# Loading most expert weight chunks as two transfers of 64 partitions in place of one of 128

## The reference

```
def expert_choice_ffn(x, router_w, wg, wu, wd):
    cap = CAPACITY_FACTOR * n // N_EXPERTS            # 32 tokens for each of 16 experts
    aff = softmax(x @ router_w); gate, idx = top_k(aff.T, cap)
    xg = x[idx]
    hid = silu(xg @ wg[e]) * (xg @ wu[e])             # 32 x 1024, for every expert e
    o = (hid @ wd[e]) * gate
    return zeros_like(x).at[idx].add(o)
```

## Time and profile before

| what | value |
|---|---|
| median of three runs | 2420.06 us |
| the profiled execution's own time | 2413.2 us |
| its span, first to last instruction | 2411.4 us |
| TensorE busy | 2212.5 us, 92% of the span |
| mean rate of all transfers over the span | 274 GB/s |
| TensorE's mean granted clock | 0.992 of full speed |
| moved | 660.65 MB |

### The profile page before, as it was taken

One profiled execution on the slowest core, in us unless ns is written; L12 is line 12 of the kernel. 1 busy time (PEld: TensorE's weight loads), 2 busy tenths in 40 slices (PEclk: granted clock), 3 DMA queues, 4 the chain that ended last, 5 costly groups with the idle time before them and its releaser, 6 DMA issues.

```text
span 2411.4 us, 28597 instructions
## 1 busy us (share of the span) xinstructions
PE 2212.5 (92%) x12096; PEld 1470.3 (61%) x12096; DVE 1111.8 (46%) x1655; ACT 840.0 (35%) x1206; POOL 46.5 (2%) x76
## 2 busy tenths in 40 slices
PE   6999999888888899999887779999999999999997
PEld 3865773324232586722231216889898888888887
DVE  4535551102010576501010106758877577758765
ACT  4425421001000355210000005544655455546544
POOL 0012000000000002000000000000000000000000
PEclk9999999999999999999999999999999999999999
DMA  8374369999999641599999997446264454455442
GB/s 332 123 309 200 150 279 408 427 428 428 428 428 428 273 159 68 212 421 428 427 428 427 428 426 288 180 168 232 91 240 166 168 210 177 164 195 207 153 169 85
DMA packets 66095, 660.65 MB, mean 274 GB/s; under 512 B 7280, under 2 KB 10352, under 8 KB 20912
## 3 DMA queue, kind: packets, MB, share of 16 engines
q1 hardware_dynamic: 65968, 658.82, 67.1%
HBM read 657.75 MB, written 1.05 MB: 273 GB/s over the span
## 4 chain that ended last, share of the span: by engine, by line
PE 69%; DMA 23%; DVE 4%; ACT 2%; issue 1%; SPq 0%; DVEq 0%; ACTq 0%
PE ps L849 20%; PE ps L1257 12%; PE ps L850 10%; DMA ring<-in_exp_up 9%; PE ps L819 5%; PE ps L820 5%; PE ps L821 5%; DMA ring_top<-in_exp_up 5%; DMA ring<-in_exp_gate 4%; DMA ring_top<-in_exp_down 2%; DMA ring<-in_exp_down 2%; PE ps L1250 2%; PE ps L872 1%; PE ps L1000 1%; DMA ring<-in_ada_w 1%
## 5 line engine op out<-in xcount | busy, mean ns | idle before, releaser
L1257 PE MATMUL ps<-ring,arena 128*32 128x512 f32 (+1 forms) x1168 | 262.7, 595 | 51.3 <-DMA ring<-in_exp_up 27.2
L849 PE MATMUL ps<-h_buf_r,ring_r 128*128 128x512 f32 x832 | 292.6, 397 | 2.9 <-DVE h_buf_r L698 2.9
L2494 DVE TENSOR_TENSOR h_buf<-h_buf,ps 128x512 f32<-128x512 f32 (+1 forms) x32 | 21.9, 683 | 497.2 <-PE ps L1257 497.2
L1257 PE MATMUL ps<-ring_top,arena 128*64 128x512 f32 (+1 forms) x848 | 190.3, 595 | 35.0 <-DMA ring_top<-in_exp_up 19.1
L1257 PEld LDWEIGHTS ps<-ring,arena 128*32 128x32 f32 (+1 forms) x1168 | 72.0, 123 | 237.3 <-issue 145.6
L850 PE MATMUL ps<-h_buf_r,ring_r 128*128 128x256 f32 x768 | 214.4, 279 | 0.0
L849 PE MATMUL ps<-h_buf_r,ring_top_r 128*128 128x512 f32 x576 | 201.8, 396 | 1.5 <-DVE h_buf_r L698 1.5
L458 DVE TENSOR_TENSOR ring_r<-ring,ring_r 128x2048 fp32r<-128x2048 f32 (+3 forms) x82 | 168.8, 2096 | 46.4 <-ACT ring_r L450 46.4
L849 PEld LDWEIGHTS ps<-h_buf_r,ring_r 128*128 128x128 f32 x832 | 156.8, 189 | 40.2 <-issue 3.1
L850 PE MATMUL ps<-h_buf_r,ring_top_r 128*128 128x256 f32 x640 | 178.0, 278 | 0.0
L2504 DVE COPY arena<-ps 32x512 f32<-32x512 f32 x48 | 33.1, 689 | 271.0 <-PE ps L1257 270.8
(11 more groups left out here) (350 smaller groups left out, 4208.5 us busy)
## 6 DMA issues: line engine op xcount, KB each, us to landing
ring<-in_exp_gate SPq DMA_DIRECT2D x40, 2048.0 KB, 27.0
ring<-in_exp_down SPq DMA_DIRECT2D x33, 2048.0 KB, 29.6
ring<-in_exp_up SPq DMA_DIRECT2D x32, 2048.0 KB, 30.5
ring_top<-in_exp_up SPq DMA_DIRECT2D x29, 2048.0 KB, 29.4
ring_top<-in_exp_down SPq DMA_DIRECT2D x27, 2048.0 KB, 28.7
ring<-in_ffn_w SPq DMA_DIRECT2D x48, 1024.0 KB, 6.8
ring_top<-in_exp_gate SPq DMA_DIRECT2D x23, 2048.0 KB, 30.2
ring_top<-in_ffn_w SPq DMA_DIRECT2D x40, 1024.0 KB, 6.8
```

The source lines that it names most:

```text
L849: release(pe.matmul(ps[:, bank, :], w[0][:, lo:lo + P], both, start=start, stop=False, skip_group_check=True))
L1257: mm = pe.matmul(out, stationary, slot(c)[:, at:at + 512], start=start, stop=stop)
```

## The change

The chunks of experts 0 to 14 in both layers are marked BY_ROWS, (2, 0): two transfers, nothing split. The last expert's chunks stay PLAIN. In load, a chunk of an expert tensor with two transfers is issued as partitions 0 to 63 and then partitions 64 to 127, each 64 rows of 16 KB, 1 MB, with the same semaphore. The bytes, their places in HBM and in the memory, and the wait for the slot are as before; the readers wait for 32 more on the semaphore in place of 16.

```
-        PLAIN, HALVED = (1, 0), (1, SLOT)
+        PLAIN, HALVED, BY_ROWS = (1, 0), (1, SLOT), (2, 0)
...
-            stream(("experts", l), *[PLAIN] * 6 * (EARLY_PLE + 1))
+            stream(("experts", l), *[BY_ROWS] * 6 * (EARLY_PLE + 1))
...
-                stream(("expert", l, e), *[PLAIN] * 6)
+                stream(("expert", l, e), *[BY_ROWS] * 6 if e < EXPERTS - 1 else [PLAIN] * 6)
...
-                    sp.dma_start(slot(n)[:, lo:lo + width], src).then_inc(slot_loaded[slot_of[n]][j], 16)
+                    if name.startswith("exp_") and loads[n] == 2:
+                        for rows_ in (slice(0, P // 2), slice(P // 2, P)):
+                            sp.dma_start(slot(n)[rows_, lo:lo + width], src[rows_, :]).then_inc(slot_loaded[slot_of[n]][j], 16)
+                    else:
+                        sp.dma_start(slot(n)[:, lo:lo + width], src).then_inc(slot_loaded[slot_of[n]][j], 16)
```

## The result

The changed kernel takes 3239.18 us (median of 4 runs, 3227.52 to 3245.91), the kernel before 2419.34 us beside it (2413.29 to 2421.56). The ratio is 1.3406, with a 95% interval of 1.3373 to 1.3439. The change costs 820 us; 3194 was forecast, with 3080 to 3290 as the likeliest case's own range.

What follows compares the result with a forecast made beforehand. The prediction took the experts to be bound by transfers at 428 GB/s. 764 us for slower chunks plus 10 for TensorE's clock on 2413 gave 3187, and 7 us of offset made 3194 us, range 2415 to 3300.

Steps and rivals of the forecast that it cites:

- What bounds the kernel: Experts of both layers: they run at the transfers' speed, 4.90 us per chunk at 428 GB/s against 3.65 us of products.
- (a) Issue: SyncE in the experts: a second issue of 0.33 us per chunk is hidden by its waits; 0 taken, 59 us without cover.
- (b) Completions: Transfer ends on the DMA engines: completion packets double, at most 0.08 us per chunk; 0 taken, 14 us kept.
- (c) The place: Memory's write side in the experts: each transfer writes half the height, at about half rate; 9.5 us per chunk taken.
- The hole of the earlier trace: Setup's table expand, 64 partitions: rate dips to 314 GB/s between 9.1 and 10.5 us, read as 1.7 to 2.2 times the cost.
- The sum: Both layers' expert queues without a gap: 174c - 889 with c us per split chunk; +764 us for c = 9.5.
- (d) The clock: TensorE, waiting more, may fall to 1.2 GHz, showing only in each layer's last expert; 0 to 29 us, 10 taken.
- (e) The tables: Layer 1's attention tables, issued 6.4 us behind chunk 0, would wait for it; 0 taken, up to 3 us kept.
- Drift as a cure: Experts' transfers: engines drift apart into different halves, halving the loss, 7.35 us per chunk; 2820 us (2500 to 3050), chance 0.20.
- No limit by height: Memory's write side: 428 GB/s is what 16 engines move wherever they write; 2420 us (2416 to 2426), chance 0.22.
- The number of transfers: Experts' transfers: only their doubled count costs, through completion packets, 14 us; 2434 us, chance 0.05.
- Worse than double: Experts' transfers: the factor 2.2 holds for large ones too, 10.8 us per chunk, +990; 3420 us, chance 0.05.

Runs made afterwards that it cites:

- even and odd kernel: Against the changed kernel, each chunk's two transfers take the even and the odd partitions; 2414.77 us beside 2415.57 for the kernel before, ratio 1.0002.
- halves alone: No model, only transfers, 12 chunks per phase: partitions 0 to 63 and 64 to 127 in turn; 210 GB/s.
- quarters: Against the changed kernel, each chunk of experts 0 to 14 is four transfers of 32 partitions; 3234.32 us (one run), 221 GB/s.
- every eighth partition: No model, only transfers, 12 chunks per phase: each takes every eighth of the 128 partitions; 210 GB/s.
- three parts: No model, only transfers: partitions 0 to 31, 32 to 95, 96 to 127, 222 GB/s; the same cut in the whole kernel, 3072.16 us, 235 GB/s.

## Why the prediction was right, and where its sizes were off

**What bounds the kernel.** Right: the rate of the transfers in the expert stages is nearly the whole effect, 805 of 814 us. The 814.3 us between the two profiled executions' spans (3225.7 and 2411.4) divide up, by the landing of chunk 95 and the issue of chunk 3, as follows (us, rounded to 0.1).

| stretch | before | after | difference | forecast |
|---|---|---|---|---|
| start to chunk 95 of layer 0 | 804.8 | 1218.7 | 413.9 | 399 |
| from there to chunk 3 of layer 1 | 180.6 | 188.2 | 7.6 | 0 |
| chunk 3 to chunk 95 of layer 1 | 474.5 | 865.2 | 390.7 | 365 |
| to the end | 951.5 | 953.5 | 2.0 | 0 |
| clock | | | in the rows above | 10 |

**(a) Issue: 0, right.** The even and odd kernel issues as many transfers, and its time is that of the kernel before within 0.2%.

**(b) Completions: 0 taken, up to 14 kept; none measured**, by the same kernel.

**(c) The place: right in kind, a little small.** 9.5 us per chunk was taken. In layer 0, where chunk 1 is now issued at 325.6 us and the rate steps up at 1187.5, it is (1187.5 - 325.6)/89 = 9.7; in layer 1 (865.2 - 32.4)/85 = 9.8. The step that was off is the deduction of 0.3 us, with its reason that two engines in different halves are both at full speed. The engines do get apart: the 16 increments of one transfer are spread over 1.9 us at 449 us and over 3.6 us at 902 us (901.8 to 905.4). But the rate stays at 218, and with 8 engines a whole transfer ahead it is 222, where halves alone get 210. So being in different halves gains a few per cent at most. The 0.2 and 0.3 us make 16 and 25 us, 41 of the 50 by which 814.3 exceeds 764; the rest is in the second and fourth row of the table. The hole of the earlier trace rows, 1.7 to 2.2 times, was a true sign: alone, partitions 0 to 63 cost 428/206 = 2.1 times. The reason given, half the height, was the coarse form of the rule; quarters, 32 to 95 and every eighth partition show that what counts is how many separate ways the rows of one transfer reach.

**The sum.** Its form held: the queue had no gap, and the earlier trace rows gave its two starting points.

**(d) The clock: fell as said, cost nothing that shows.** It is 0.78 and 0.75 in the two stages, where TensorE is busy 62% of the time. In the last experts it is 0.96 and 0.89, and the transfers there are still at 422 and 410 GB/s, so TensorE never became the limit. The 10 us were too many. The sign "TensorE's wait from 1.3 to over 5" was missed for the same reason: the wait is 4.3 us, because the products take 5.35 us at this clock.

**(e) The tables: 6.4 us, taken as 0, with 3 kept as the most.** The bound was wrong: it counted only what chunk 0 takes beyond the tables' issue, some 3.3 us (9.7 less 6.4). Why the attention lost 6.4 us was not tried; that it came of chunks 0 to 2 is shown.

**The rivals.** Drift as a cure is out: the engines do drift, and a forced lead of half a chunk lasts, but neither that nor two queues brings the rate back. No limit by height is out at 218 GB/s. The number of transfers is out by the even and odd partitions. Worse than double is out.

**Still open.** In "three parts" the middle transfer should have run at the full rate between the outer ones, as it does alone (431); in the mixture the mean is 222, and 235 in the whole kernel. Nor is it explained why the halves don't add up when 8 engines write one and 8 the other (222), or when both are in flight on two queues (224). The traces don't say which engine writes which partitions, so which engines share a way is not known; they may be two of the same group of 8. That crowded writes hold up others behind them is a guess. Nor is it explained why even and odd partitions stay at 430: if an engine takes four neighbouring rows of the transfer (not shown), pairs of engines should share ways there too.

## What to carry to other kernels

Cut a transfer that the kernel waits for so that each piece still reaches all the ways into the memory. By columns (0.45% here, with rows of 8 KB) or by even and odd partitions (nothing) is harmless, where partitions 0 to 63 and 64 to 127 halve the rate although both are queued together. Each transfer counts by itself: a second queue or a lead between the engines didn't make up for one that reaches half the ways. If the profile shows a stage at a constant 428 GB/s with no free time on the DMA engines, look at every edit by what it does to the rate, not to the issue or the wait. And a slower transfer can cost time through its neighbours in the queue, even where nobody waits for the transfer itself: 6.4 us ahead of layer 1's experts.

## What had not been expected of the hardware

- A quarter (partitions 0 to 31) is as fast as a half (0 to 63): 205 and 206 GB/s. 16 neighbouring partitions get 117, and 64 in the middle 431.
- The engines don't keep in step, and it gains next to nothing. One transfer's 16 increments are spread over 3.6 us in the changed kernel and over 4.1 us in the one before (702.6 to 706.7), each in a cycle of 4.9 us. A forced lead of half a chunk lasts for over 40 chunks, at 222 GB/s.
- A second queue didn't mend it: 224 GB/s with a half on each queue, 272 with the middle half on one and the outer quarters on the other, against 430.
- TensorE fell to a granted clock of 0.75 to 0.78 when it waited about 4.3 us of every 9.7; in the last expert, where it was busy for 24 of 28 and of 30 us, it had 0.96 and 0.89.
